# Probabilities normalised before their transposes, a value matmul with V stationary, other PSUM banks in the router, and weight splits placed earlier

## What is computed

```python
for l in range(DEPTH):                      # DEPTH = 2
    h = rmsnorm(x, attn_norm_g[l])
    z = h @ w_in[l] + b_in[l]               # moba q,k,v; gla q,k,v,a,r; mlstm q,k,v,i,f,o; 3 gates
    # softmax attention: 8 heads of 64, 256 tokens, query blocks of 128, causal
    p = softmax(where(causal, q @ k.T * HD**-0.5, -inf)); y_moba = p @ v
    # gated linear attention and mLSTM (its q, k go through a depthwise conv of 4 taps and silu)
    y_gla = rms(gla(...)) * g * silu(r); y_mlstm = mlstm(silu(conv(q)), silu(conv(k)), v, i, f) * sigmoid(o)
    merged = g0*(y_moba @ w_up_moba) + g1*(y_gla @ w_up_gla) + g2*(y_mlstm @ w_up_mlstm)
    x = x + merged @ w_o[l]
    x = x + (swiglu(...) if l == 0 else moe(...))
# moe: logits = xt @ router_w + router_b; top 2; softmax over the two; rank of each token
# within its expert; per expert (silu(x_e @ w_gate) * (x_e @ w_up)) @ w_down, gated and added back
return rmsnorm(x, final_norm_g)
```

## Time and profile before

| | before |
|---|---|
| median of 3 runs | 1545.37 us (1543.23 to 1545.9) |
| the profiled execution's own time | 1545.86 us |
| its span in the profile | 1544.1 us |
| PE busy | 1516.3 us, 98% of the span |
| PEld / DVE / ACT busy | 1267.2 / 1231.9 / 946.0 us |
| DMA | 412.71 MB, mean 267 GB/s; over the experts mostly 320 to 380 GB/s |
| chain that ended last | PE 91%, DVE 5%, ACT 2% |

### The profile page before, as it was taken

How to read it: one execution, slowest core, us unless ns; L and a number is a source line. 1 busy time by engine, 2 the same in 40 slices (tenths; PEclk the granted TensorE clock), 3 DMA queues, 4 the chain that set the end, 5 groups by cost and what they waited for, 6 DMA issues and landing times.

```text
span 1544.1 us, 19326 instructions
## 1 busy us (share of the span) xinstructions
PE 1516.3 (98%) x7534; PEld 1267.2 (82%) x7534; DVE 1231.9 (80%) x1218; ACT 946.0 (61%) x881; POOL 37.9 (2%) x69
## 2 busy tenths in 40 slices
PE   8999999999999999999899999999999999999996
PEld 6898888888888898888678888888888888888885
DVE  5778876655547688866699998989989999899996
ACT  6347534544435356534677777777777777777775
POOL 2000000000000000001000000000000000000000
PEclk9999999999999999999999999999999999999998
DMA  8544545455554455546799998999989999999980
GB/s 297 212 166 141 191 175 191 174 189 191 191 191 166 177 184 183 180 164 242 308 367 377 348 372 327 360 376 347 372 321 372 370 353 355 341 363 370 351 305 29
DMA packets 114802, 412.71 MB, mean 267 GB/s; under 512 B 13264, under 2 KB 13568, under 8 KB 114704
## 3 DMA queue, kind: packets, MB, share of 16 engines
q1 hardware_dynamic: 111872, 402.52, 69.7%
q0 software_dynamic: 2688, 8.61, 1.7%
q10 hardware_dynamic: 144, 0.26, 0.0%
HBM read 410.29 MB, written 1.05 MB: 266 GB/s over the span
## 4 chain that ended last, share of the span: by engine, by line
PE 91%; DVE 5%; ACT 2%; issue 1%; DMA 1%; SPq 0%; DVEq 0%; ACTq 0%
PE ps L1100 31%; PE ps L665 19%; PE ps L1111 14%; PE ps L966 8%; PE ps L655 4%; PE ps L943 4%; PE ps L644 3%; DVE w_lo L1665 2%; PE ps L1054 1%; DMA raw_m<-dense_dram 1%; PE ps L1078 1%; DVE w_lo L1521 1%; PE ps L1063 1%; ACT w_hi L1179 1%; PE ps L623 0%
## 5 line engine op out<-in xcount | busy, mean ns | idle before, releaser
L1665 DVE TENSOR_TENSOR w_lo<-late,w_hi 128x2048 fp32r<-128x2048 f32 x192 | 438.1, 2290 | 38.7 <-ACT w_hi L1241 38.6
L1241 ACT CAST w_hi<-late 128x2048 fp32r<-128x2048 f32 x192 | 367.3, 1913 | 44.3 <-PE ps L1100 44.3
L1521 DVE TENSOR_TENSOR w_lo<-raw_m,w_hi 128x2048 fp32r<-128x2048 f32 x115 | 262.6, 2290 | 130.7 <-ACT w_hi L1179 130.4
L1179 ACT CAST w_hi<-raw_m 128x2048 fp32r<-128x2048 f32 x115 | 218.2, 1906 | 132.7 <-PE ps L665 54.7
L1100 PE MATMUL ps<-w_hi,hT_hi 128*128 128x512 f32 x704 | 281.9, 400 | 2.3 <-DVE w_lo L1665 2.3
L1100 PE MATMUL ps<-w_hi,hT_lo 128*128 128x512 f32 x704 | 274.9, 390 | 0.0
L1100 PE MATMUL ps<-w_lo,hT_hi 128*128 128x512 f32 x704 | 274.6, 390 | 0.0
L665 PE MATMUL ps<-w_hi,hT_hi 128*128 128x512 f32 x464 | 183.6, 396 | 3.5 <-DVE w_lo L1521 3.5
L1665 DVE TENSOR_TENSOR w_lo<-raw_m,w_hi 128x2048 fp32r<-128x2048 f32 x72 | 165.4, 2298 | 24.2 <-ACT w_hi L1241 24.2
L665 PE MATMUL ps<-w_hi,hT_lo 128*128 128x512 f32 x464 | 181.0, 390 | 0.0
L665 PE MATMUL ps<-w_lo,hT_hi 128*128 128x512 f32 x464 | 180.7, 389 | 0.0
(11 more groups left out here) (343 smaller groups left out, 2158.2 us busy)
## 6 DMA issues: line engine op xcount, KB each, us to landing
late<-experts_dram SPq DMA_DIRECT2D x384, 512.0 KB, 4.7
raw_m<-dense_dram SPq DMA_DIRECT2D x233, 512.0 KB, 4.0
raw_m<-experts_dram SPq DMA_DIRECT2D x144, 512.0 KB, 4.4
bias<-b_in_dram POOLq DMA_DIRECT2D x26, 256.0 KB, 4.8
xt<-x_dram SPq DMA_DIRECT2D x4, 256.0 KB, 8.2
tmp<-front_dram SPq DMA_DIRECT2D x3, 256.0 KB, 6.3
out_dram<-xn SPq DMA_DIRECT2D x3, 256.0 KB, 4.2
tmp<-w_small_dram POOLq DMA_DIRECT2D x2, 320.0 KB, 5.1
```

The lines of the kernel that those rows point to most:

```text
L1179: copy(w_hi[:, g % RS, :], slot_raw(g, False)).then_inc(hi_ready, 1)
L1241: copy(w_hi[:, m % RS, :], slot_raw(m, True)).then_inc(hi_ready, 1)
L1521: tt(w_lo[:, g % RS, :], slot_raw(g, False), w_hi[:, g % RS, :], ALU.subtract)\
L1665: tt(w_lo[:, m % RS, :], slot_raw(m, True), w_hi[:, m % RS, :], ALU.subtract).then_inc(lo_ready, 1)
```

## The change

- Attention: `row_sums` also divides the probabilities by their sums (two multiplications over 128x1024 and 128x512 per group, semaphore `p_scaled`). `prob_transposes` waits for that; the second group's fourth head is transposed after chunk 0 of lo. `prob_values` has V (128x64) stationary and pT moving, so that yT comes out directly, two heads on the two halves of the partitions, in one bank (4 and 5). `moba_rows` and `y_transposes(l, 0)` go; ScalarE and VectorE write yT_hi and yT_lo from the two banks at once.
- Order in the mixers: chunk 0 of lk is split ahead of row_sums(0); lo's second `ahead` stands ahead of the scans; `conv_taps(l, 1)` moves from in front of the lo rows to behind the g0' rows, its silu to behind `ahead(l, "up0")`.
- Dense FFN: layer 1's first split comes behind the last yT_lo.
- Router: logits in bank 2, ranks in bank 4, ten keep_warm ahead of the claim in place of five behind it.
- Experts: only (gu, 0, 1) of expert 1 and later is late. add_rows(t = 0) moves from behind (gu, 1, 0) to behind hid of (gu, 1, 1). gates_of_picks moves from (dn, 2) to step 1.

The diff, cut:

```diff
-    fills(1, "logits", (0,))
+    fills(1, "logits", (2,))
     fills(1, "lgT", (1,))
-    fills(1, "rank", (0,))
+    fills(1, "rank", (4,))
...
-            def prob_transposes(l, g):
-                pe.wait_ge(p_ready, 2 * l + g + 1)
-                for hh in range(4):
+            def prob_transposes(l, g, heads):
+                pe.wait_ge(p_scaled, 2 * l + g + 1)
+                for hh in heads:
...
+                b = claim(l, f"pv{g}")
                 for hh in range(4):
...
+                    p0, c0, v = HD * (hh % 2), hh // 2 * T, slice((4 * g + hh) * HD, (4 * g + hh + 1) * HD)
+                    mm(ps[p0:p0 + HD, b, c0:c0 + T], vm[:, 0, v], pT[:, hh, 0:T], start=True, stop=False,
+                       skip_group_check=True)
+                    ins = mm(ps[p0:p0 + HD, b, c0 + P:c0 + T], vm[:, 1, v], pT[:, hh, T:T + P], start=False, stop=True,
+                             skip_group_check=True)
...
-                prob_transposes(l, 1)
-                unit(l, "lo")
+                prob_transposes(l, 1, range(3))
+                chunk(l, "lo", 0)
+                prob_transposes(l, 1, (3,))
+                chunk(l, "lo", 1)
...
                 chunk(l, "g0'", 0)
-                y_transposes(l, 0)
                 chunk(l, "g0'", 1)
...
+            keep_warm(10)
             lg_bank = claim(1, "logits")
-            keep_warm(5)
...
-                ahead(l, "gr")
+                ahead(l, "lq", 0)
                 act.wait_ge(sub_ready, 2 * l + 2)
...
+                tt(sc[:, g, :, 0:T], sc[:, g, :, 0:T], sums[:, g, 1, :].unsqueeze(2).to_broadcast([P, 4, T]), ALU.mult)
+                tt(sc[:, g, :, T:T + P], sc[:, g, :, T:T + P], sums[:, g, 0, :].unsqueeze(2).to_broadcast([P, 4, P]),
+                   ALU.mult).then_inc(p_scaled, 1)
...
-                            split_to(min(2 * NU + n + 2, LAYER_BASE[1]))
+                            split_to(min(2 * NU + n + 2, LAYER_BASE[1] - 1))
...
-                    late_split = kind == "gu" and c == 1 and i < 2
+                    late_split = e > 0 and (kind, i, c) == ("gu", 0, 1)
...
+                    if pas == 0 and m == 1:
+                        gates_of_picks()
...
+                        if e and i == 1:
+                            add_rows(pas, e - 1, 0)
...
-                    if e and (kind, i, c) == ("gu", 1, 0):
-                        add_rows(pas, e - 1, 0)
...
-                            gates_of_picks()
```

## The result

| | before | after |
|---|---|---|
| median | 1545.05 us (1543.23 to 1545.9, 4 runs) | 1530.07 us (1529.11 to 1531.04, 4 runs) |
| ratio after / before | | 0.9905, 95% interval [0.9887, 0.9922] |
| profiled execution: own time, span | 1545.86, 1544.1 us | 1530.97, 1529.2 us |

The changed kernel is 15.0 us (0.95%) faster, 0.6 us from the forecast of 1529.5.

The account below looks back on a forecast made before the run. TensorE, busy 1516.3 of 1544.1 us, was taken to set the time. Gains of 5.5 + 4.0 + 1.6 + 0.9 + 2.9 + 1.0 = 15.9 us from the 1545.37 median gave 1529.5, range 1526 to 1536.

Parts of the forecast that it names:

- The router: Router and gather: hole ahead of the gather goes, clock stays up, first expert matmul starts 5.5 us earlier.
- The logits' wait: Router: logits no longer wait for wo' additions to drain bank 0; 0.35 us less, bounds 0 and 0.7.
- Of which 2.9 are the clock: Gather to first expert matmul: 2.9 of the router's 5.5 us come from full instead of half clock.
- the serial rival: Attention: value matmuls run one after another, 2.6 us a group; 4.0 us less gained, 1533.5; chance 0.13.
- Nearest to the scores: Value matmuls, side by side in array halves, were priced like the score matmuls: 1.6 us a group, 4.0 us gained.
- The transposes: Mixers: eight y transposes go per layer, one slower start is added; net 0.8 us per layer, 1.6 in all.
- in the sum the new waits cost 0: Mixers: VectorE's added multiplications and new order cost TensorE nothing, with thin cover.
- The two places I had named: Mixers' tight places: split of g0' chunk 0, 0.3 us to spare, and y_ready, 1.0 us to spare.
- The end of the FFN: Dense FFN: yT_lo no longer stands behind a split, so its wait goes; 0.9 us less.
- The rival, that the wait would only change its name: Experts: the wait goes to hid of chunk 2, splits gain nothing; 2.9 us less gained, 1532.4; chance 0.10.
- Expert 0: Expert 0: waits of 0.42 (two) and 1.03 us go, a new one of about 0.8 comes; 1.0 us less.
- the third rival: Mixers' new order makes waits, costing up to 4.1 us per layer, 8.2: 1533 to 1538; chance 0.12.

Follow-up runs that it names:

- the filled hole: Kernel before with 34 keep_warm in place of 7 behind the ranks, the gather still waiting for its bank: 1543.34 us, 0.9983 of before.
- the experiment with one half: Changed kernel with all four heads' value matmuls on the same half of the array's columns: 1534.25 us, 0.9927 of before.

## Why the prediction came out

**The router: right, but for 0.3 us behind the last copy.** It was 5.24 us against 5.5. The logits' wait brought the 0.35 that I took: TensorE is 0.9 us earlier at the first keep_warm, but then waits for VectorE's rows as before (the row of 0.8 on L1564 is still in the list), and the second half of the logits, at 740.26 before and at 736.28 now, is 0.35 earlier than the shift of 3.63 us that all the stages ahead had brought. The gather started 3.2 us earlier on the same count; I had 3.3, and it starts 0.06 us behind the selection matrix (741.21 + 0.69). The clock stayed up. The end of the stage was, as forecast, VectorE's second copy of a lo group, made as soon as VectorE was free: it ends at 746.09, which is 749.72 on before's time, and I had 749.8. But TensorE starts 0.37 us behind it, as it had before (754.96, then 755.32), and that step I had at nothing. "Of which 2.9 are the clock" was too large by 0.7, as the filled hole shows; the 5.5 doesn't hang on it, since it was counted to the copy. The waits for banks 6 and 7, 0.4 us and a little in the forecast, hardly came (two starts 0.20 us apart in place of 0.12), and TensorE's end of the gather was not what came last.

**The value matmuls: right, by the reason given.** 1.51 us a group against 1.6, and the experiment with one half gives 2.75 for the serial rival's 2.6, with 0.65 a head. "Nearest to the scores" was the right choice of row. The gain at the spot was 4.4 us.

**The transposes: 0.7 in each layer, where 0.8 was forecast.** The eight that went and the slower start behind them gave 0.85 (g0' with them took 11.91 us from first to next, now 11.06). The second group's twelve with unit lo cost 0.19 more in two pieces (12.24, now 12.43), twice what I took for it.

**The mixers as a sum: 1.0 us too much.** 4.6 came of 5.6. The step that failed is "in the sum the new waits cost 0". The two places I had named behaved: the split of g0' chunk 0 ended at 154.63 in a profile that runs 1.59 us later from mv on, so at 153.04 on before's time, where I had 153.0; y_ready stood at 183.9 where I had 183.7. TensorE waited at neither. What I hadn't looked at is what stands behind that split in VectorE's order and is wanted sooner than it: lcol's copy, and the bank that it frees. It cost 0.87 us in each layer, 1.7 in all (3.96 us from the first score matmul to g0' where it was 3.09). The sum is off by less because of gains that I had at nothing: two short holes of before, 0.14 us ahead of lk and 0.20 inside g0, are gone in each layer (probably by the earlier splits; no run shows them apart), and the value matmuls gave 0.4 more in all. My rule was to ask of each split whether it comes late; I should have asked it of each instruction queued behind one.

**The end of the FFN: 0.6 against 0.9.** The wait went as described, and a small one came that no row explains.

**Experts 1 to 7: 3.4 against 2.9.** The stage gave 0.45 to 0.53 each, where I had 0.42. I had allowed 0.22 us for the two transposes of 865.18. Where TensorE doesn't wait they take 0.14, as the next ones of before show, so the wait cost 0.50:

```profile
875.07 0.38 PE L1078 MATMUL ps<-ident,ytok 128*128 128x128 f32 x2
875.21 0.48 PE L1100 MATMUL ps<-w_hi,hT_hi 128*128 128x512 f32 x1
```

The rival, that the wait would only change its name, did not come, with hid done 0.44 us ahead of its reader.

**Expert 0: 1.2 against 1.0**, with the new wait at its place. It is 0.84 us in the list, forecast at 0.8, and costs 0.96 by the starts (746.46 to 755.71, where the same work took 8.29 before); the two old waits that went gave 0.50 each and not 0.42.

**Where errors met.** The mixers were 1.0 us over, the FFN's end 0.3 and the router 0.3; the experts were 0.7 under. That left 0.9 us in a sum of 15.9. That they met is luck, and so is a part of the 0.6 us of the median: I had taken the 15.9 from 1545.37, the median of three executions of before, and with the fourth it is 1545.05. In the profiled execution of before the odd start and end (+1.6, -1.4) would have hidden more than all of these, had they not met each other. The 8.2 us of the third rival, the mixers' new waits, make 1537.7 and not 1537.5; the range had left that part out in either case.

## What to carry to other kernels

A hole on TensorE is worth its length plus what runs at half clock behind it: the 3.06 us hole cost 2.2 more, one of 2.05 cost 3.0 more, so the first holes to remove are those after which the granted clock falls. When a split or another slow step waits for a second engine, look at what is queued behind it that was ready already, and move the small instructions that free a bank in front; here one moved line was worth 1.5 us by the median. Small matmuls that fill half of the array's columns should alternate between the halves from one head to the next: here they gained nothing on the same half.

## What the runs showed of the hardware

- Value matmuls in fp32 with 128 rows and 64 columns: a head (256 + 128 columns, two passes each) takes 0.65 us, two heads on different halves of the columns take that together, and two on the same half twice that. In the order 0, 2, 1, 3 only the two neighbours on different halves overlapped: 1.51, 2.15 and 2.75 us for the same 16 passes.
- Behind 2.05 us of idle time on TensorE, with full work before it, the granted clock was 0.50, as it was behind the 3.06 us of before; behind the 0.8 us between the logits it stayed at 1.00 in every profile.
- The gather's matmuls of 256 columns started 0.213 us apart at a granted clock of 0.50 and 0.120 at 1.00, so half the clock was not twice the time.
- The start of this kernel is not the same from run to run: the clock fell there or did not, and the first chunks end up to 2.1 us apart between profiles of kernels that are the same up to that point. Of a change of 2 us the trace tells more if one compares stretches that leave out both ends.
